# Eight half tiles of an output product between the blocks of a gated linear attention, with the gating run two blocks late

## The reference

```python
def hybrid_mixer(h, w_in, pool_w, pool_scale, gk_w2, gk_b, gla_norm_w, w_out):
    proj = h @ w_in
    p, q, k, v, g_low, r = ...                       # columns of proj
    pool_out = multiscale_pool(p, pool_w, pool_scale)        # 512 wide
    log_g = log_sigmoid(g_low @ gk_w2 + gk_b) / 16
    o = gla_chunked(heads(q, 64), heads(k, 64), heads(v, 128), heads(log_g, 64))
    o = rms_norm_2(o, gla_norm_w)                    # over the 128 of a head
    gla_out = o * silu(r)                            # 512 wide
    return concatenate([pool_out, gla_out], -1) @ w_out
```

## Time and profile before

| what | value |
|---|---|
| median of 3 runs | 2642.59 us (2641.2 to 2642.66) |
| span of the profiled execution | 2639.0 us |
| time of the profiled execution beside its span | not given |
| PE busy | 2551.3 us (97%) |
| DVE busy | 1402.0 us (53%) |
| ACT busy | 749.6 us (28%) |
| POOL busy | 102.1 us (4%) |

### The profile page before, as it was taken

One profiled execution on the slowest core, in us unless ns is written; L12 is line 12 of the kernel. 1 busy time (PEld: TensorE's weight loads), 2 busy tenths in 40 slices (PEclk: granted clock), 3 DMA queues, 4 the chain that ended last, 5 costly groups with the idle time before them and its releaser, 6 DMA issues.

```text
span 2639.0 us, 32575 instructions
## 1 busy us (share of the span) xinstructions
PE 2551.3 (97%) x11931; PEld 2096.2 (79%) x11931; DVE 1402.0 (53%) x2180; ACT 749.6 (28%) x1407; POOL 102.1 (4%) x100
## 2 busy tenths in 40 slices
PE   6999999999999999999998899989999999999997
PEld 5868888888788878788786688888888888888886
DVE  6436666666552243345464634474487437743763
ACT  4223333434441121232143232253322112211223
POOL 4000000000000000021000020000100000000000
PEclk8999999999999999999998699999999999999999
DMA  5111111111111121131110012310111111111112
GB/s 170 48 32 49 40 48 40 40 48 40 53 49 49 48 104 48 58 101 52 40 48 24 1 48 64 112 48 25 40 56 48 48 48 48 48 48 48 48 52 76
DMA packets 233403, 140.66 MB, mean 53 GB/s; under 512 B 4382, under 2 KB 228787, under 8 KB 232322
## 3 DMA queue, kind: packets, MB, share of 16 engines
q1 hardware_dynamic: 230258, 125.36, 16.2%
q0 software_dynamic: 3088, 14.54, 1.6%
HBM read 127.30 MB, written 12.58 MB: 53 GB/s over the span
## 4 chain that ended last, share of the span: by engine, by line
PE 91%; DVE 5%; ACT 2%; DMA 1%; issue 1%; SPq 0%; DVEq 0%; ACTq 0%
PE bank L680 27%; PE bank L682 27%; PE bank L681 27%; PE bank L771 1%; PE bank L759 1%; PE bank L732 1%; DVE wlo L1521 1%; PE bank L760 1%; PE bank L761 1%; PE bank L783 1%; PE bank L785 1%; PE bank L784 1%; PE bank L920 1%; PE bank L910 1%; DVE R L1932 0%
## 5 line engine op out<-in xcount | busy, mean ns | idle before, releaser
L680 PE MATMUL bank<-xhi,whi 128*128 128x512 f32 x1088 | 425.4, 391 | 9.6 <-DVE xt L1552 8.4
L681 PE MATMUL bank<-xlo,whi 128*128 128x512 f32 x1088 | 424.3, 390 | 0.0
L682 PE MATMUL bank<-xhi,wlo 128*128 128x512 f32 x1088 | 424.1, 390 | 0.0
L1104 ACT ACTIVATE whi<-wraw 128x1024 fp32r<-128x1024 f32 x158 | 166.8, 1056 | 689.7 <-PE bank L682 689.3
L1521 DVE TENSOR_TENSOR wlo<-wraw,whi 128x1024 fp32r<-128x1024 f32 x217 | 267.7, 1234 | 119.1 <-ACT whi L1104 76.9
L680 PE MATMUL bank<-x4hi,whi 128*128 128x512 f32 x704 | 274.3, 390 | 0.0
L682 PE MATMUL bank<-x4hi,wlo 128*128 128x512 f32 x704 | 273.9, 389 | 0.0
L681 PE MATMUL bank<-x4lo,whi 128*128 128x512 f32 x704 | 273.9, 389 | 0.0
L680 PEld LDWEIGHTS bank<-xhi,whi 128*128 128x128 f32 x1088 | 204.9, 188 | 53.7 <-DVE xt L1552 8.8
L681 PEld LDWEIGHTS bank<-xlo,whi 128*128 128x128 f32 x1088 | 204.8, 188 | 42.8 <-issue 0.2
L682 PEld LDWEIGHTS bank<-xhi,wlo 128*128 128x128 f32 x1088 | 204.8, 188 | 42.8
(11 more groups left out here) (336 smaller groups left out, 4674.0 us busy)
## 6 DMA issues: line engine op xcount, KB each, us to landing
wraw<-in_w_in_dram SPq DMA_DIRECT2D x85, 512.0 KB, 3.8
wraw<-in_ffn_w_up_dram SPq DMA_DIRECT2D x44, 512.0 KB, 3.8
wraw<-in_w_out_dram SPq DMA_DIRECT2D x16, 512.0 KB, 4.1
wraw<-in_xattn_wkv_dram SPq DMA_DIRECT2D x16, 512.0 KB, 3.9
wraw<-in_ffn_w_down_dram SPq DMA_DIRECT2D x16, 512.0 KB, 4.1
xraw<-in_x_dram SPq DMA_DIRECT2D x4, 1024.0 KB, 7.9
x_spill<-xt SPq DMA_DIRECT2D x8, 512.0 KB, 6.3
conv_spill<-tv POOLq DMA_DIRECT2D x8, 512.0 KB, 3.2
```

Of the source, the lines that this page charges most:

```text
L680: pe.matmul(acc, whi[slot][:, k, :], xh, start=(k == 0), stop=False)
L681: pe.matmul(acc, whi[slot][:, k, :], xl, start=False, stop=False)
L682: last = pe.matmul(acc, wlo[slot][:, k, :], xh, start=False, stop=(k == k_tiles - 1))
L1104: act.activation(whi[slot][:, :, :], wraw[slot][:, :, :], ACT.Copy).then_inc(s_whi, 1)
```

## The change

1. The output product is done in 16 half products instead of 8 whole ones. For each of the 8 output tiles, the product with the 4 pooled pieces (tiles T_W2P) and that with the 4 pieces of the linear attention (tiles T_WO2) are accumulated apart, and both are added to the residual. Weight loads and splits are half as large and twice as many.
2. The 8 pooled tiles stand on PE one after each block of the recurrence.
3. Gating runs up to two blocks late, with three `go` buffers.
4. The sum of squares has the squares as weights and one column of ones per head, which gives 128 tokens on the partitions by 4 heads. ACT takes the root of 128x4, DVE the reciprocal of 128x4 and a 128x512 product with the identity (`gla_diag`), and PE spreads it over the partitions with ones (`gla_spread`).
5. `gla_out` and `gla_kv` run their matmuls in another order, so that neighbours use different halves of the array's rows.
6. The gate work of the projection stage comes one tile earlier, tanh goes to SBUF instead of PSUM, PSUM banks are assigned anew, and `xq32`, `x3lo`, `xohi`, `xolo` change places in SBUF.

```diff
-T_WO2 = T_R + 4
+T_W2P = T_R + 4
+T_WO2 = T_W2P + 8
...
-            loads(T_WO2, 8, (w, 0, 2), (w, 1, 2))
+            for t, w in ((T_W2P, tiles(w_out_2[0, 0:4 * P, :])), (T_WO2, tiles(w_out_2[0, 4 * P:8 * P, :]))):
+                loads(t, 8, (w, 0, 2), (w, 1, 2))
...
-                for h in range(4):
-                    q, m = 64 * (h % 2), h // 2
-                    pe.matmul(bank[0][:, h % 2, m * P:(m + 1) * P], gvt[b % 2][:, h * P:(h + 1) * P],
-                              gst[b % 2][:, h % 2, m, :], start=True, stop=False, skip_group_check=True)
+                for m in range(2):
+                    for q in range(2):
+                        h = 2 * m + q
+                        pe.matmul(bank[2][:, q, m * P:(m + 1) * P], gvt[b % 2][:, h * P:(h + 1) * P],
+                                  gst[b % 2][:, q, m, :], start=True, stop=False, skip_group_check=True)
                     for c in range(2):
                         lo = m * P + c * CHUNK
                         tok = b * P + c * CHUNK
-                        last = pe.matmul(bank[0][:, h % 2, lo:lo + CHUNK], gss[b % 2][q:q + 64, c, m, :],
-                                         qk32[q:q + 64, m, tok:tok + CHUNK], start=False, stop=(c == 1),
-                                         skip_group_check=True)
+                        for q in range(2):
+                            last = pe.matmul(bank[2][:, q, lo:lo + CHUNK], gss[b % 2][64 * q:64 * q + 64, c, m, :],
+                                             qk32[64 * q:64 * q + 64, m, tok:tok + CHUNK], start=False,
+                                             stop=(c == 1), skip_group_check=True)
...
             def gla_sum(b):
 
                 pe.wait_ge(s_gla_o_copied, b + 1)
+                for h in range(4):
+                    last = pe.matmul(bank[2][:, 0, 2 * P + h:2 * P + h + 1], gosq[:, h, :], ones[:, 0:1],
+                                     start=True, stop=True)
+                last.then_inc(s_gla_o_sum, 1)
+
+            def gla_spread(b):
+
+                pe.wait_ge(s_gla_diag, b + 1)
                 if b:
                     pe.wait_ge(s_gla_gated, b)
-                pe.matmul(ps(5), ones[:, :], gosq[:, :, :].rearrange("p q n -> p (q n)"), start=True, stop=True)\
-                    .then_inc(s_gla_o_sum, 1)
-
-            pe.wait_ge(s_free, 2 * T_WO2)
+                pe.matmul(ps(1), ones[:, :], R[:, 0:HALF], start=True, stop=True).then_inc(s_gla_spread, 1)
+
+            def part(t, h, acc, hi, lo, sem, value):
+
+                slot = t % 2
+                pe.wait_ge(s_wlo, t + 1)
+                for k in range(4):
+                    pe.wait_ge(sem, value if value else k + 1)
...
+            def pool_half(t, h):
+
+                if t > T_W2P:
+                    pe.wait_ge(s_free, 2 * (t - 1) + h + 1)
+                part(t, h, ps(2 + h), phi, plo, s_concat_lo, None)
...
             for b in range(NB):
+                if b:
+                    pool_half(T_W2P + b - 1, 0)
+                    pool_half(T_W2P + b - 1, 1)
+                    gla_sum(b - 1)
                 if b + 1 < NB:
                     gla_turn(b + 1)
+                if b >= 2:
+                    gla_spread(b - 2)
                 gla_out(b)
                 if b + 1 < NB:
                     gla_scores(b + 1)
                     gla_kv(b + 1)
-                gla_sum(b)
...
+            t = T_W2P + NB - 1
+            pool_half(t, 0)
+            gla_spread(NB - 2)
+            gla_sum(NB - 1)
+            pool_half(t, 1)
+            gla_spread(NB - 1)
+            for h in range(2):
+                pe.wait_ge(s_free, 2 * t + h + 1)
+                part(T_WO2, h, ps(2 + h), glahi, glalo, s_gla_lo, NB // 2 * (h + 1))
```

The last part of the diff is the order on DVE:

```diff
+            for b in range(1, NB):
+                gla_mask(b)
+                gla_state(b)
+                if b == 1:
+                    silu(T_W2P - 1)
+                for h in range(2):
+                    add_result(T_W2P + b - 1, b - 1, h, ps(2 + h))
+                split(T_W2P + b + 1, (T_W2P + b + 1) % 2)
+                gla_diag(b - 1)
+                if b >= 2:
+                    gla_gate(b - 2)
+                    gla_lo(b - 2)
```

More of the change, by code:

```diff
@@ L178, in hybrid_then_mixer_kernel @@
         rcnt = at("rcnt", [P, 16], F32, late + 672)
+        groot = at("gla_root", [P, 4], F32, late + 736)
+        ginv = at("gla_inverse", [P, 4], F32, late + 768)
         TMP = top[0]
@@ L854, in _ @@
             dense(T_QK + 1, (T_QK + 1) % 2, x2hi, x2lo)
-            with pe.Fori(0, (T_WO2 - T_QK - 2) // 2) as i:
+            with pe.Fori(0, (T_W2P - T_QK - 2) // 2) as i:
                 for j in range(2):
@@ L935, in _ @@
                     gla_kv(b + 1)
-                gla_sum(b)
-            pe.wait_ge(s_gla_o_copied, NB)
-            with pe.Fori(0, 4) as i:
-                for j in range(2):
-                    dense(2 * i + (T_WO2 + j), (T_WO2 + j) % 2, c2hi, c2lo,
-                          ready=lambda k, h: None if h else (s_concat_lo, k + 1) if k < 4 else (s_gla_lo, NB))
+            t = T_W2P + NB - 1
[7 more added lines that the diff above has]
+                part(T_WO2, h, ps(2 + h), glahi, glalo, s_gla_lo, NB // 2 * (h + 1))
+            pe.wait_ge(s_gla_gated, NB)
+            for t in range(T_WO2 + 1, T_XQ):
+                for h in range(2):
+                    if t > T_WO2 + 1:
+                        pe.wait_ge(s_free, 2 * t + (h - 3))
+                    part(t, h, ps(2 * (t % 2) + h), glahi, glalo, s_gla_lo, NB)
             def mem_tile(t, slot):
@@ L1315, in gate_exps @@
                     act.activation(gk[:, m, half], gk[:, m, half], ACT.Exp, scale=1.0 / 16).then_inc(s_gk_exp, 1)
[L1317 removed]
+            for n in range(T_QK + 1, T_W2P):
                 split(n + 2, n % 2)
[L1319 removed]
+                if n == T_QK + 1:
                     log_gates(0)
+                if n == T_QK + 3:
+                    gate_exps(0)
                 if n == T_V:
[L1322 to L1323 removed]
                     log_gates(1)
[L1325 removed]
+                if n == T_V + 2:
                     gate_exps(1)
@@ L1965, in _ @@
-            pooled_lo(2)
-            gla_lo(NB - 1)
-            pooled_lo(3)
-            residual(2, T_WO2, x3hi, x3lo, PCOL["norm_xattn_w_2"])
+            split(T_W2P + 1, (T_W2P + 1) % 2)
+            for g in range(4):
+                pooled_lo(g)
+            for b in range(1, NB):
+                gla_mask(b)
+                gla_state(b)
+                if b == 1:
+                    silu(T_W2P - 1)
+                for h in range(2):
+                    add_result(T_W2P + b - 1, b - 1, h, ps(2 + h))
+                split(T_W2P + b + 1, (T_W2P + b + 1) % 2)
+                gla_diag(b - 1)
+                if b >= 2:
+                    gla_gate(b - 2)
+                    gla_lo(b - 2)
@@ new lines, in _ @@
+            t = T_W2P + NB - 1
+            add_result(t, NB - 1, 0, ps(2))
+            gla_gate(NB - 2)
+            gla_diag(NB - 1)
+            gla_lo(NB - 2)
+            add_result(t, NB - 1, 1, ps(3))
+            split(T_WO2 + 1, (T_WO2 + 1) % 2)
+            gla_gate(NB - 1)
+            gla_lo(NB - 1)
+            for f in range(KT):
+                t, slot = T_WO2 + f, (T_WO2 + f) % 2
+                for h in range(2):
+                    add_result(t, f, h, ps(2 * slot + h))
+                split(t + 2, slot)
+                lower(2, f, resid, x3hi, x3lo, f + PCOL["norm_xattn_w_2"])
```

195 lines of the change are left out of this document (107 added, 88 removed).

## The result

The changed kernel takes 2599.2 us in the median of four runs (2597.06 to 2600.78), against 2641.89 us for the kernel before in the same sitting: a ratio of 0.9839, with a 95% interval of 0.9825 to 0.9852. That is 42.7 us less. The prediction was 2611 us, 31.6 us less than the 2642.59 it started from, with a range down to 2600; the measured time lies just under that range. So the direction was right, and the gain was underestimated by a quarter. The profiled execution took 2600.78 us with a span of 2599.2 us.

The account below looks back on a forecast made before the run. PE was taken to set the end, slowed by waits and a low clock. For the stretch, 87.0 + 52.6 + 3.0 + 1.5 + 8 = 152.1 us against 183.8; span 2607.3, plus 3.6 gives 2611, range 2600 to 2630.

Parts of the forecast that it names:

- (1): Output product: split in halves it stays at 384 matmuls, 87.0 us, nothing gained or lost on PE.
- (2): Recurrence: a block's reordered output takes 2.8 us instead of 4.0, with full-array records 1.68 and state records 1.1.
- (3) to (5): Other small work per block: narrow sum 0.96 us, spreading 0.96, turning 0.55, scores 0.6, k-v 0.7.
- (6): Recurrence loop: PE waits for nothing, DVE has 7.0 of 12.0 us a round, 2.5 us to spare at the tightest place.
- (7): Start of the recurrence: the silu and mask waits go, two new waits of about 1.5 us each come, 3.0.
- (8): End of the recurrence: waits of 0.2 us before the last spreading and 1.2 in T_WO2's first tile, taken as 1.5.
- (9): The seven tiles after the recurrence, 5.44 us each: work of DVE, ACT and POOL stays hidden behind PE.
- (10): Granted clock: the lower level costs 5 us at the start and 3 us over eight rounds (0 to 33).
- B: Rival, chance 0.16: dearer small matmuls, pairing fails (+9.4 us) or the narrow sum costs as 128 columns (+5.9); 2621 us.
- C: Rival, chance 0.12: without gaps, most blocks' output, scores and k-v still run at 1.2 GHz; 2641 us for all eight.

Follow-up runs that it names:

- e3_no_pairs: The changed kernel with each head pair's state products ordered by head, so that neighbours use the same half of the rows; 2600.71 us.
- e4_one_behind: The changed kernel with spreading and gating one block late instead of two; 2651.64 us.
- e6: e5_wide_root with `gla_out` and `gla_kv` in their old orders, leaving interleaving, half tiles and part 6; 2612.07 us.
- e10: e1 with the output head by head in its old order, nothing interleaved; 2650.21 us over twelve runs.
- e12: e10 with the first two pooled tiles put back between the blocks; 2634.71 us over ten runs.
- e1: The changed kernel with all eight pooled tiles, their additions and weight splits moved behind the recurrence; 2608.0 us.
- e2: The changed kernel with the output products in the old order, head by head; 2615.17 us.
- e5_wide_root: The changed kernel with the old norm (sum with 128x128 ones, root and reciprocal of 128x512) and gating one block late; 2600.43 us.
- e8: The kernel before with only the new order of the output's matmuls; 2630.73 us.
- e9_full_then_half: The changed kernel with a block's four full-array output products before all eight state products, output not the reference's; 2595.7 us.
- e7_ends: The changed kernel with ACT's first copy ahead of a weight split and two tanh, and DVE's last gating ahead of a weight split; 2595.6 us.
- e11_grouped_ends: e7_ends plus the grouping of e9_full_then_half, without the second accumulation start, output the reference's; 2591.51 us.

## Why the prediction was right or wrong

The sum of the stretch was 152.1 us and it is 143.3, so 8.8 of the 11.8 us by which the median was missed lie there. The prediction also kept 3.6 us between span and median; the profiled execution's own time is 1.6 over its span (2600.78 and 2599.2), and the median of the runs is at the span. That offset was taken from one span and a median of other runs, and its 3.6 us went into the number without a mechanism. In the later runs of the kernel before, a run's time lies 1.5 to 2.4 us above its own span. The rest of the kernel gave 0.7 back.

- **(1) 384 matmuls in 87.0 us**: right but for the entry. A pooled tile behind small work costs 5.57 instead of 5.44, 1.0 us over eight.
- **(2) Output, 4.0 to 2.8: the step that failed most.** Measured 2.26, so 4.3 us of the 8.8. The records with the states cost what I took (0.60 and 0.49 for 1.1). The eight full-array ones were kept at 1.68, 0.21 each, because two of them took 0.42; they take 1.17 (0.53 and 0.64). Half of that 0.42 was the change of form, not the records, and the rows of before showed groups of one size only. Neighbours on different halves, the reason I gave for the states, are not what does it (e3_no_pairs): that price was right for a reason that was so only in part. The Trainium skill ("TensorEngine Tiling (Array Packing)", Key Properties) says that changing the tiling mode drains TensorE. Reading full and half array as two modes, the 0.33 us a change agrees with it, and the prediction didn't look for it.
- **(3) to (5)**: narrow sum 0.80 for 0.96, spreading 0.86 for 0.96, turning 0.70 for 0.55, scores and k-v 0.60 each for 0.6 and 0.7. With the output the small work is 5.82 a block for 6.57: 6.0 us over eight, the largest part of the miss.
- **(6) No wait in the loop**: right. PE has none from 1430 to 1500. I put the first addition at 10.8 after the end of a pooled tile; it came at 9.2 to 9.9 in the trace. The distance of two blocks is what covers the small root: with one block less PE waits 3.0 us a round and the kernel is 52 us slower (e4_one_behind). With two, that chain has some 8.4 us to spare, an estimate (a round of 11.4 less those 3.0).
- **(7), (8) Ends**: 2.6 and 0.8 us for 3.0 and 1.5. The wait of 0.2 before the last spreading did not occur.
- **(9)** Nothing waits in the last seven tiles: right.
- **(10) Clock**: 4.2 us at the start for 5 (output 2.0, scores and k-v 1.0, dense product 1.2), none in the loop for 3. The reasoning behind the 3 took the 0.62 of the earlier trace rows for a danger of all small work. It belongs to the old order (e6, e10 and e12 against e1). The term was a guess between 0 and 33, and the 0 it came to is owed to the order of the output, which had been priced for PE's time alone: with the old order the clock falls in some rounds in spite of the interleaving (e2, e6).

The terms give 6.0 + 3 + 0.8 + 0.4 + 0.7 - 1.0 = 9.9, one more than the 8.8 that are missing. Part of that one are the last records before the three waits, which take 0.1 to 0.2 us longer where nothing follows them at once; the rest I can't place.

Of the rivals, B fell on both of its points. C named a real thing, the clock falling in gapless small work, and missed that the loops in the new order without long waits don't do it. The trace of before had the sign of it: between 1456.6 and 1492 PE waits for nothing, and there the clock falls twice, near 1462 and near 1473, each time at the end of an output. The first of them in its timeline: a head's records at the upper clock, and the scores 1.8 us later at the lower.

```profile
1460.54 0.49 PE L905 MATMUL bank<-gst,gvt 128*128 128x128 f32 x2
1460.96 0.66 PE L910 MATMUL bank<-qk,gss 64*128 64x64 f32 x4
...
1462.74 1.21 PE L879 MATMUL bank<-qk 64*128 64x128 f32 x5
```

Behind rival C I had cited the Trainium skill ("TensorE: Matmul & The Clock Gate", A second HAM failure mode), by which short idles between groups make the clock swing. The traces here do not agree: e5_wide_root idles up to 1.1 us in five rounds and stays up, e10_behind_by_head idles nowhere in its rounds and stays down.

What the parts are worth, then. Interleaving with part 6 gives 30 us (e6). The order of the output gives 9 on the old kernel (e8), 12 to 16 beside the interleaving (e6 against e5, e2), 42 in the median without it (e10 against e1), most of it through the clock. The small root and late gating give nothing in themselves (e5), and without the new order and the interleaving nothing that the runs could tell (e10, 0.9992 to 1.0042). Part 5's new order of `gla_kv` was not tried apart.

## What to carry to other kernels

Price a small matmul from groups of at least two lengths with the same kind of work behind them, so that the cost of changing between full and half array separates from that of a record; then put all full-array products of a step together and all half-array ones together. Before filling gaps with dense work, look whether the clock falls where there are none: here it was then the small work's own order that had to change. A reduction to a narrow form moves the load off one engine but adds a round trip, and the distance in blocks that hides it has to be worked out with the same care as the load.

## What the runs showed of the hardware that was not expected

- The granted clock can fall to 1.2 GHz, and stay there for 100 us, while PE is busy in every window and waits for nothing (e10_behind_by_head, 1416 to 1517.7); the same matmuls in another order bring it back in 17 us (e1_pooled_behind). It isn't so in every execution: three of twelve took 2625 to 2629 us, and in e12_two_tiles_early the clock came back after 7 us, in the old order. It fell in that order at the end of an output, with no wait near, in the traces of before, e6_interleave_alone and e12_two_tiles_early. What the clock reacts to in the old order was not isolated. The old order has twice as many changes between full and half array, with PE shown as busy during them, and it runs one half of the rows with the other one idle; that either is the cause is argued, not shown.
- A gap of 3.0 us lost the clock every round, dense tiles notwithstanding (e4_one_behind), and gaps of 2.5 to 2.7 us lost it in the new order too (e8_order_on_before). A gap of 1.6 us there and those of up to 1.1 us in e5_wide_root did not. In the kernel before the clock fell at a wait of 1.2 us (1455.5) and not at one of 1.4 (1447.4), so these lengths are no bound.
- Behind the same two waits of 1.3 us at the start, the clock fell in the changed kernel's trace (0.73 in 1410 to 1420) and stayed at 1.00 in that of e9_full_then_half. The runs of one kernel differ in the same way by their mean clock: e7_ends took 2593 at 0.991 and 2602 at 0.985, e11_grouped_ends 2590.5 to 2591.5 and 2596.4 to 2596.8. That it is the start that differs between those runs is argued; one run of each was traced.
- A float32 product with one column of 128x128 weights takes 0.20 us in a row of four, two records each.
